# A hybrid diffusion block on one core: modulation and norm in one stage, four modulation rows moved beside the gate projection

## The chip, the cores and the metric

The kernel runs on one core of one Trainium2 chip. Its time is the device time of one execution in microseconds (us), the median of several runs. The core has five engines with queues of their own: TensorE (PE; PEld is its weight load), VectorE (DVE), ScalarE (ACT), GpSimd (POOL) and SyncE (SP, which here only issues DMAs). They wait for each other through semaphores.

## The reference, cut to what matters

The block takes 1024 latent tokens and 256 context tokens of width 1024. Two vectors, `c` for the latents and `c_ctx` for the context, are turned into modulation vectors; the normed tokens are scaled and shifted with them, and one large projection feeds the mixers that follow.

```python
mod = silu(c) @ w_ada + b_ada            # 6 * 1024 values
mod_c = silu(c_ctx) @ w_ada + b_ada
sh1, sc1, g1, sh2, sc2, g2 = split(mod, 6)
csh1, csc1, ... = split(mod_c, 6)
h  = layer_norm(x)   * (1 + sc1)  + sh1
hc = layer_norm(ctx) * (1 + csc1) + csh1
p, pc = h @ w_in, hc @ w_in              # conv channels, q and k, gates, z, v, dt
...                                      # two mixers, merge
x = layer_norm_affine(alpha * x + g1 * y)
h = layer_norm(x) * (1 + sc2) + sh2      # then experts, and g2 in the second residual
```

Only `sh1`, `sc1` and their context twins are needed before the projection. The four vectors `g1`, `sh2`, `sc2`, `g2` are read much later (L2079, L2293), and only those of the latents.

## The kernel before, in words

The program is a row of stages. Each is a block in which every engine has its own program, and a barrier of all engines stands between two stages. The change touches the first three.

`adaln_stage` computes the first 2048 columns of the modulation for `c` and `c_ctx`. `w_ada` comes in four blocks of 512 columns (2 MB each, two buffers). TensorE takes the two silu vectors as stationary (128x2) and streams the weights (L188), so the result is two rows. VectorE adds the bias (L199), GpSimd stores the rows to HBM as `mod` (L205).

`norm_stage` reads these rows back as 32x128, turns them into columns with one transpose (L360), and then works through ten tiles of 128 tokens, two buffers each. For a tile, VectorE takes mean and variance (L302 to L308), ScalarE the root (L340), VectorE normalises (L312), TensorE transposes eight 128x128 squares (L373), VectorE multiplies and adds the modulation columns (L326, L328), ScalarE rounds the result to fp32r, `h_hi` (L345), and VectorE keeps the remainder `h_lo` (L332). Beside the eight latent tiles TensorE computes eight more blocks of 512 modulation columns (L366, L367), ScalarE copies them out (L349), GpSimd stores them (L393).

`project_f_stage` multiplies `w_in` by the tokens: 24 chunks of 128 channels for the convolution, 10 for q and k, 16 for the gates. A chunk's weights (512 KB) come through SP (L465) into one of two buffers; the load waits until the chunk two before has been split. ScalarE rounds them to `w_hi` (L543) once the product two chunks before is done, VectorE keeps `w_lo` (L616), and TensorE makes three passes, hi*hi, hi*lo and lo*hi (L482). For a gate chunk ScalarE applies the Sigmoid (L575) after it has rounded the next chunk's weights, and GpSimd stores it (L685). VectorE does nothing in a gate chunk but the split.

All order is written out by hand in each engine's program, and a queue is served strictly in that order.

Of the kernel before, what the change touches and what calls it, by code (L numbers as in the profile page):

```python
# [23 lines left out]
P = 128  # L24
# [117 lines left out]
def adaln_stage(s, mod):  # L142
# [3 lines left out]
    NB = 2 * D // 512  # L146
    with ExitStack() as st:
        cond = own(st, nc, "cond", [P, 2, KT])
        act_c = own(st, nc, "act_c", [P, 2, KT])
        w = own(st, nc, "w_ada_t", [P, 2, KT, 512])  # L150
        bias = own(st, nc, "b_ada_t", [2, 2 * D])
        row = own(st, nc, "mod_row", [2, 2 * D])
        acc = bank(st, nc, "mod_acc", [P, 2, 512])
        cond_in, bias_in, silu_done = s.sem("cond_in"), s.sem("bias_in"), s.sem("cond_silu")
        w_in = [s.sem(f"ada_w_in{b}") for b in range(2)]

        w_free, acc_free = s.sem("ada_w_free"), s.sem("mod_acc_free")
        stored = s.sem("mod_stored")

        wv = s.x["w_ada"][0].rearrange("(p k) n -> p k n", k=KT)  # L160
        with nc.Block() as block:

            @block.sync
            def _(sp):
                sp.dma_start(cond[:, 0, :], s.x["c"][0].rearrange("(p k) -> p k", k=KT)).then_inc(cond_in, 16)
                sp.dma_start(cond[:, 1, :], s.x["c_ctx"].rearrange("(p k) -> p k", k=KT)).then_inc(cond_in, 16)
                for r in range(2):
                    sp.dma_start(bias[r:r + 1, :], s.x["b_ada"][:, 0:2 * D]).then_inc(bias_in, 16)
                with sp.Fori(0, NB // 2) as i:
                    for b in range(2):  # L170
                        sp.wait_ge(w_free, 2 * i + b + 1)
                        sp.dma_start(w[:, b], wv[:, :, ds(1024 * i + 512 * b, 512)]).then_inc(w_in[b], 16)

            @block.scalar
            def _(act):
                act.wait_ge(cond_in, 32)
                nc.scalar.activation(act_c[:], cond[:], ACT.Silu).then_inc(silu_done, 1)

            @block.tensor
            def _(pe):  # L180
                pe.sem_inc(w_free, 2)
                pe.wait_ge(silu_done, 1)
                with pe.Fori(0, NB // 2) as i:
                    for b in range(2):
                        pe.wait_ge(w_in[b], 16 * i + 16)
                        pe.wait_ge(acc_free, 2 * i + b + 1)
                        for k in range(KT):
# [2528 lines left out]
```

## Time and profile before

| | us |
|---|---|
| median of 3 runs | 3188.68 |
| lowest, highest | 3185.52, 3190.0 |
| the profiled execution | 3189.44 |
| its span | 3187.70 |
| TensorE busy | 2554.5 (80%) |
| VectorE busy | 1654.8 (52%) |
| ScalarE busy | 1024.8 (32%) |
| GpSimd busy | 649.5 (20%) |

In 40 slices of the span (79.7 us each) TensorE's busy share and its granted clock read, in tenths (9 is 90% or more):

```profile
PE   5799999999799747695899669696763888788792
PEclk8999999999899868897999879798876999999996
```

The two stages that become one take nearly the first two slices; slices 9 to 11 hold the gate chunks. The span is measured from the first to the last event of the program, and the execution's own time is 1.74 us longer.

### The profile page before, as it was taken

Reading aid. Unit: us, or ns where it says so; the run is one execution under the profiler, and the core shown is the slowest. Engines: PE = TensorE matmul, PEld = TensorE weight load, DVE = VectorE, ACT = ScalarE, POOL = GpSimd, SP = SyncE. Lnnn points to the kernel's source line nnn. Section 1 sums busy time; section 2 is a strip of 40 time slices with the busy share of each in tenths; the row PEclk is TensorE's granted clock in tenths of the full one; section 3 lists DMA queues with packets and bytes.
Section 4 is the critical chain, followed back from the end, with each engine's and each line's share of the span. In section 5 each row is a group of like instructions: output and inputs, shape, how many; then the busy total and the mean of one; then the engine's idle time right before and its main releaser. Section 6 shows DMA issues by size and latency. Waiting matters only on the chain. (4 is left out here: it accounts for less than half of the span.)

```text
span 3187.7 us, 31676 instructions
## 1 busy us (share of the span) xinstructions
PE 2554.5 (80%) x11173; PEld 1952.1 (61%) x11173; DVE 1654.8 (52%) x1734; ACT 1024.8 (32%) x1231; POOL 649.5 (20%) x462
## 2 busy tenths in 40 slices
PE   5799999999799747695899669696763888788792
PEld 1188888778678612464666358584652767666672
DVE  2545555431010079684566252532655877767775
ACT  0123333121121100352333331311322656555562
POOL 0100001010001149596000000000552121122212
PEclk8999999999899868897999879798876999999996
DMA  5633333343231164895433345444316887788874
GB/s 193 229 98 115 115 115 115 101 147 97 93 125 50 46 238 180 280 309 146 76 72 68 99 139 145 146 139 147 106 59 241 316 325 295 300 317 315 329 292 138
DMA packets 302209, 546.14 MB, mean 171 GB/s; under 512 B 23320, under 2 KB 196872, under 8 KB 279792
## 3 DMA queue, kind: packets, MB, share of 16 engines
q1 hardware_dynamic: 273108, 433.03, 40.3%
q0 software_dynamic: 25440, 91.10, 8.5%
q10 hardware_dynamic: 3584, 21.04, 1.7%
q8 instruction: 41, 0.67, 0.1%
q14 instruction: 36, 0.29, 0.0%
HBM read 425.78 MB, written 119.07 MB: 171 GB/s over the span
## 5 line engine op out<-in xcount | busy, mean ns | idle before, releaser
L2370 DVE TENSOR_TENSOR e_wlo<-e_w,e_whi 128x2048 fp32r<-128x2048 f32 x188 | 426.4, 2289 | 57.9 <-ACT e_whi L2323 57.8
L2323 ACT CAST e_whi<-e_w 128x2048 fp32r<-128x2048 f32 x192 | 366.4, 1915 | 130.1 <-PE e_gu L2483 82.1
L482 PE MATMUL f_lat<-h_hi,w_hi 128*128 128x512 f32 x800 | 254.2, 399 | 0.3 <-DVE w_lo L616 0.3
L482 PE MATMUL f_lat<-h_lo,w_hi 128*128 128x512 f32 x800 | 250.8, 394 | 0.0
L482 PE MATMUL f_lat<-h_hi,w_lo 128*128 128x512 f32 x800 | 250.6, 394 | 0.0
L616 DVE TENSOR_TENSOR w_lo<-w_raw,w_hi 128x1024 fp32r<-128x1024 f32 x50 | 61.2, 1225 | 216.5 <-ACT w_hi L543 216.5
L1918 PE MATMUL b_acc<-b_hi,b_whi 128*128 128x512 f32 x384 | 151.4, 394 | 14.0 <-DVE b_lo L1869 14.0
L1576 PE MATMUL a_c_ps<-a_prob,a_v 128*128 128x512 f32 x304 | 154.6, 592 | 0.0
L482 PEld LDWEIGHTS f_lat<-h_hi,w_hi 128*128 128x128 f32 x800 | 135.9, 188 | 30.4 <-issue 4.8
L482 PEld LDWEIGHTS f_lat<-h_lo,w_hi 128*128 128x128 f32 x800 | 136.0, 188 | 27.6
L482 PEld LDWEIGHTS f_lat<-h_hi,w_lo 128*128 128x128 f32 x800 | 136.0, 188 | 27.7
L629 DVE SCALAR_TENSOR_TENSOR conv_acc<-conv_in,conv_tap_cols,conv_acc 128x1284 f32<-128x1284 f32 x96 | 149.4, 1556 | 3.4
L1918 PE MATMUL b_acc<-b_lo,b_whi 128*128 128x512 f32 x384 | 151.0, 393 | 0.0
L1918 PE MATMUL b_acc<-b_hi,b_wlo 128*128 128x512 f32 x384 | 150.7, 393 | 0.0
L1645 DVE CUSTOM_DVE_ANT_0 a_masked<-a_a_ps,a_mask 128x640 f32<-128x640 f32 x128 | 105.0, 824 | 87.3 <-PE a_a_ps L1549 84.3
L749 PE MATMUL t_acc<-wt_hi,h_hi 128*128 128x512 f32 (+1 forms) x336 | 125.2, 373 | 26.2 <-DVE wt_lo L799 26.2
L2483 PE MATMUL e_gu<-e_whi,e_xhi 128*128 128x512 f32 x512 | 140.3, 396 | 3.2 <-DVE e_xlo L2374 2.4
L2483 PE MATMUL e_gu<-e_wlo,e_xhi 128*128 128x512 f32 x512 | 138.7, 393 | 0.0
L2483 PE MATMUL e_gu<-e_whi,e_xlo 128*128 128x512 f32 x512 | 137.5, 390 | 0.0
L1615 ACT ACTIVATE a_prob<-a_b_ps 128x512 f32<-128x512 f32 x152 | 89.2, 597 | 148.4 <-PE a_b_ps L1565 74.5
L2543 POOL DMA_INDIRECT moe<-e_y,e_scatter_rows x16 | 43.9, 2741 | 429.9 <-DVE e_y L2391 429.9
L749 PE MATMUL t_acc<-wt_hi,h_lo 128*128 128x512 f32 (+1 forms) x336 | 124.8, 372 | 0.0
(323 smaller groups left out, 5313.4 us busy)
## 6 DMA issues: line engine op xcount, KB each, us to landing
e_w<-in_w_gate_up SPq DMA_DIRECT2D x128, 1024.0 KB, 8.5
e_w<-in_w_down SPq DMA_DIRECT2D x64, 1024.0 KB, 5.3
w_raw<-in_w_in SPq DMA_DIRECT2D x50, 512.0 KB, 3.9
w_ada<-in_w_ada SPq DMA_DIRECT2D x8, 2048.0 KB
before<-s_state ACTq DMA_DIRECT2D x16, 1024.0 KB, 3.9
y_before<-before SPq DMA_DIRECT2D x64, 256.0 KB, 6.1
b_w<-in_w_ssd_br SPq DMA_DIRECT2D x16, 1024.0 KB, 5.6
xbcF<-f_out POOLq DMA_DIRECT2D x24, 640.0 KB, 3.4
```

The costliest lines, as they stand in the source:

```text
L482: mm = nc.tensor.matmul(o, weights[:, b, k, :], part[:, k, a:a + n], start=(k == 0 and n_pass == 0), stop=(k == KT - 1 and n_pass == 2))
L616: nc.vector.tensor_tensor(wlo[:, b], w[:, b], whi[:, b].bitcast(F32), ALU.subtract).then_inc(w_free, 1)
L629: nc.vector.scalar_tensor_tensor(conv[:, b], padded[:, b, c:c + W_OUT], tap[:, b, c:c + 1], conv[:, b], ALU.mult, ALU.add).then_inc(conv_s ...
L749: mm = nc.tensor.matmul(acc[:, t % 8, 0:width], part[:, k, a:a + P], weights[:, b, k, 0:width], start=(k == 0 and n_pass == 0), stop=(k == ...
L1576: nc.tensor.matmul(out, values(v, c, g), prob[:, T % PR], start=first, stop=last).then_inc(tiles_summed, 1)
L1615: nc.scalar.activation(prob[:, T % PR], b_ps[:, T % 2], ACT.Exp, scale=SCALE).then_inc(exps_made, 1)
L1645: V.tensor_tensor_reduce(masked[:, h % 2], a_ps[:, h % 2, A0:A0 + KEYS], mask[:, variant(m)], 1.0, NEG, ALU.add, ALU.max, top[:, h:h + 1]) ...
L1918: mm = nc.tensor.matmul(acc[:, b, j], weights[:, b, k, :], xpart[:, k, :], start=(k == ks[0] and n_pass == 0), stop=(k == ks[-1] and n_pas ...
L2323: nc.scalar.copy(whi[:, slot % SPLIT], w[:, slot]).then_inc(w_hi, 1)
L2370: V.tensor_tensor(wlo[:, slot % SPLIT], w[:, slot], whi[:, slot % SPLIT].bitcast(F32), ALU.subtract).then_inc(w_split, 1)
L2483: mm = nc.tensor.matmul(gu[:, 512 * c:512 * c + 512], part[:, b, k, :], weights[:, slot % SPLIT, 512 * c:512 * c + 512], start=(k == 0 and ...
L2543: pool.indirect_dma_start(moe, bass.IndirectOffsetOnAxis(ap=scatter_rows[:, 0:1], axis=0), y[:, b], None, compute_op=ALU.add).then_inc(y_o ...
```

## The change

`adaln_stage` and `norm_stage` become one `front_stage`. All loads are issued at once: four 2 MB blocks of `w_ada`, ten tiles of tokens, each with a place of its own. The modulation is computed the other way round: the weights are the stationary operand (128x128) and the two silu vectors the moving one (128x2), so that it comes out as columns and needs neither HBM nor a transpose. VectorE normalises all ten tiles first, then modulates them with eight instructions of 128x128 per tile, each a multiply and an add with two columns as scalars. ScalarE rounds; the remainder is taken by GpSimd for seven tiles and by VectorE for tiles 2, 5 and 8. Three buffers hold `h` and the transposes.

The four later vectors move into `project_f_stage`, beside the gate chunks, for `c` alone. VectorE adds up `w_ada[:, k] * silu(c)[k]` over eight pieces of 128x1024 (512 KB each, loaded by SP), TensorE sums over partitions with a column of ones, VectorE adds the bias into a row, and SP stores it. Two pieces are handled per gate chunk, a row is finished after chunks 5, 9, 13 and 15 (counted from 0). SP's and TensorE's loops over gate chunks are written out.

```diff
-def adaln_stage(s, mod):
+def front_stage(s, hi, lo):
...
+                load_x(0)
+                load_w(0)
+                sp.dma_start(bias[:], s.x["b_ada"][:, 0:2 * D]).then_inc(bias_in, 16)
+                sp.dma_start(ident[:], s.squares[:, 0:P]).then_inc(ident_in, 16)
+                load_x(1)
+                load_x(2)
+                load_w(1)
+                load_x(3)
+                load_x(4)
+                load_w(2)
+                load_x(5)
+                load_w(3)
+                for n in range(6, NCHUNK):
+                    load_x(n)
...
+                def mods(b):
+                    pe.wait_ge(w_in[b], 16)
+                    for t in range(NT):
+                        kind, j = divmod(b * NT + t, KT)
+                        cols = slice(P * t, P * t + P)
+                        for k in range(KT):
+                            nc.tensor.matmul(mod_ps[:, kind, j, :], w[:, b, k, cols], act_c[:, :, k], start=(k == 0), stop=False)
+                        mm = nc.tensor.matmul(mod_ps[:, kind, j, :], bias[:, 512 * b + P * t:512 * b + P * t + P], ones[:], start=False, stop=True)
+                    mm.then_inc(mods_made, 1)
...
+                for b in range(BLOCKS):
+                    mods(b)
+                    if b < TR:
+                        turn(b)
+                for n in range(TR, NCHUNK):
+                    turn(n)
...
+                centre(NCHUNK - 1)
+                dve.wait_ge(mods_made, BLOCKS)
...
+                    for k in range(KT):
+                        V.tensor_scalar(h[:, n % TR, k, :], tp[:, n % TR, k, :], colm[:, 1, which, k:k + 1], colm[:, 0, which, k:k + 1],
+                                        ALU.mult, ALU.add).then_inc(h_made, 1)
...
+                for n in range(NG):
+                    sp.wait_ge(w_free, NX + NQK + n + 1)
+                    sp.dma_start(w[:, n % 2], wv[:, :, G0 + P * n:G0 + P * n + P]).then_inc(w_in[n % 2], 16)
+                    if n == 0:
+                        load_rest(0)
+                        load_rest(1)
+                    if n >= 1 and 2 * n + 1 < PARTS:
+                        load_rest(2 * n)
+                        load_rest(2 * n + 1)
+                    if n >= 5 and n % 4 == 1:
+                        store_rest(n // 4 - 1)
+                store_rest(REST - 1)
...
+                for n in range(2, NG):
+                    product(NX + NQK + n, n % 2, False)
...
+                    if n >= 5 and n % 4 == 1:
+                        sum_rest(n // 4 - 1)
+                sum_rest(REST - 1)
...
+                for n in range(NG):
+                    if n >= 2:
+                        split_lo(NX + NQK + n, n % 2)
+                    add_rest(2 * n)
+                    add_rest(2 * n + 1)
+                    if n >= 5 and n % 4 == 1:
+                        make_row(n // 4 - 1)
+                make_row(REST - 1)
```

In it `load_rest(j)` loads piece j of `w_ada` into one of two buffers once VectorE has done addition j-2, `store_rest(c)` waits for `make_row(c)` and stores row c, `sum_rest(c)` is TensorE's sum of eight pieces, and `make_row(c)` waits for it.

SP in the gate chunks, before, one turn of the loop over two chunks; `w_raw` is the chunk's weights, `f_w_free` counts the splits:

```order
L465 ISA [waits f_w_free]
L465 DMA w_raw<-in_w_in 128x8x128
L464 REGISTER_ALU
L465 ISA [waits f_w_free]
L465 DMA w_raw<-in_w_in 128x8x128
L462 REGISTER_ALU
L462 COMPARE_AND_BRANCH
```

SP at chunks 5 to 7 now; `f_ada_w` is a piece of `w_ada`, `f_ada_row` the finished row, `f_ada_made` counts rows:

```order
L397 DMA w_raw<-in_w_in 128x8x128 [waits f_w_free]
L385 DMA f_ada_w<-in_w_ada 128x1024 [waits f_ada_step] x2
L393 DMA mod<-f_ada_row 1x1024 [waits f_ada_made]
L397 DMA w_raw<-in_w_in 128x8x128 [waits f_w_free]
L385 DMA f_ada_w<-in_w_ada 128x1024 [waits f_ada_step] x2
L397 DMA w_raw<-in_w_in 128x8x128 [waits f_w_free]
```

The load of chunk 6's weights has come to stand behind two loads of pieces and the store of row 0.

VectorE at the same chunks, before, with the last remainders of the keys ahead of the loop:

```order
L651 TENSOR_TENSOR qk_lo<-f_out,qk_hi 128x1280 [waits f_qk_hi_made] x2
L659 UNCONDITIONAL_BRANCH
L659 ISA
L616 TENSOR_TENSOR w_lo<-w_raw,w_hi 128x1024 [waits f_hi_made]
L615 REGISTER_ALU
L616 TENSOR_TENSOR w_lo<-w_raw,w_hi 128x1024 [waits f_hi_made]
```

And now, from chunk 5's split to chunk 6's; `f_ada_sum` is the running sum, `f_ada_summed` counts TensorE's sums:

```order
L572 TENSOR_TENSOR w_lo<-w_raw,w_hi 128x1024 [waits f_hi_made]
L625 SCALAR_TENSOR_TENSOR f_ada_sum<-f_ada_w,f_act_c,f_ada_sum 128x1024 [waits f_ada_step,f_ada_in0]
L625 SCALAR_TENSOR_TENSOR f_ada_sum<-f_ada_w,f_act_c,f_ada_sum 128x1024 [waits f_ada_step,f_ada_in1]
L632 TENSOR_TENSOR f_ada_row<-f_tp,f_ada_bias 1x1024 [waits f_ada_bias_in0,f_ada_summed]
L572 TENSOR_TENSOR w_lo<-w_raw,w_hi 128x1024 [waits f_hi_made]
```

Between two splits there are now two additions, and at this chunk the row, which waits for TensorE.

TensorE at the start of the program, now; `n_mod_ps` are the modulation columns, `n_tp` the transposes:

```order
L224 MATMUL n_mod_ps<-n_act_c,n_w 128x2 x7
L225 MATMUL n_mod_ps<-n_ones,n_bias 128x2
L224 MATMUL n_mod_ps<-n_act_c,n_w 128x2 x8
L225 MATMUL n_mod_ps<-n_ones,n_bias 128x2
...
L233 MATMUL n_tp<-n_ident,n_x 128x128 [waits n_normed]
L233 MATMUL n_tp<-n_ident,n_x 128x128 x7
L224 MATMUL n_mod_ps<-n_act_c,n_w 128x2 [waits n_w_in1]
```

Where a block of 512 columns was 8 instructions with an output of 2x512, it is now four groups of 8+1 with an output of 128x2, and a tile's transposes stand between two blocks.

## Rows read from the trace of the kernel before

**Rows 1.** The page's busy times: engine, us, share, instructions.

```profile
PE 2554.5 (80%) x11173; PEld 1952.1 (61%) x11173; DVE 1654.8 (52%) x1734; ACT 1024.8 (32%) x1231; POOL 649.5 (20%) x462
```

**Rows 2.** Stretches: length, busy of PE, PEld, DVE, ACT, POOL, clock, DMA share, GB/s.

```profile
10.00:16.40 6.40, 5.03 (x6) 0.73 (x7) 0.00 (x0) 0.00 (x0) 0.00 (x0) 1.00 0.90 343
55.00:165.00 110.00, 83.64 (x244) 26.31 (x245) 67.30 (x98) 19.49 (x31) 8.32 (x15) 0.83 0.66 228
700.00:1000.00 300.00, 273.50 (x1180) 221.81 (x1180) 33.86 (x18) 55.30 (x54) 22.24 (x42) 0.95 0.30 104
```

**Rows 3.** TensorE in order of time, front: start, us, line, names, [idle before].

```profile
11.37 16.36 PE L188 MATMUL mod_acc<-w_ada_t,act_c 128*2 128x512 f32 x32 [11.37 <-DMA w_ada_t<-in_w_ada]
29.44 13.89 PE L188 MATMUL mod_acc<-w_ada_t,act_c 128*2 128x512 f32 x32 [1.71 <-DMA w_ada_t<-in_w_ada]
...
68.49 1.97 PE L373 MATMUL ln_tp<-ident,x_norm 128*128 128x128 f32 x8 [6.29 <-DVE x_norm L312]
...
134.87 7.03 PE L366 MATMUL mod_acc<-w_ada,act_c 128*2 128x512 f32 x16
...
159.65 0.55 PE L482 MATMUL f_ctx<-h_hi,w_hi 128*128 128x256 f32 x1 [16.81 <-DVE w_lo L616]
```

**Rows 4.** The other engines in order of time, between norm and projection.

```profile
144.10 0.52 POOL L393 DMA_DIRECT2D mod<-mod_row  x1 [8.40 <-ACT mod_row L349]
...
146.86 0.33 SPq L457 DMA_DIRECT2D squares<-const_squares  x1
...
157.25 1.04 ACT L543 CAST w_hi<-w_raw 128x1024 fp32r<-128x1024 f32 x1 [13.79 <-DMA w_raw<-in_w_in]
...
158.32 1.23 DVE L616 TENSOR_TENSOR w_lo<-w_raw,w_hi 128x1024 fp32r<-128x1024 f32 x1 [1.14 <-ACT w_hi L543]
```

**Rows 5.** TensorE in order of time, residual stage.

```profile
2243.50 3.60 PE L2054 MATMUL r_logits<-r_router,r_h2F 128*128 128x16 f32 x16 [1.10 <-ACT r_h2F L2104]
...
2247.93 1.05 PE L2041 MATMUL r_acc<-r_wlo,r_mhi 128*128 128x512 f32 x2
...
2252.16 0.63 PE L2041 MATMUL r_acc<-r_whi,r_mhi 128*128 128x512 f32 x2
...
2262.50 1.96 PE L2054 MATMUL r_logits<-r_router,r_h2F 128*128 128x16 f32 x16 [1.10 <-ACT r_h2F L2104]
```

**Rows 6.** Groups by line and form: total us, mean ns of one | idle before.

```profile
L326 DVE TENSOR_TENSOR h_full<-ln_tp,mod_cols 128x1024 f32<-128x1024 f32 x10 | 12.2, 1224 | 0.6 <-PE ln_tp L373 0.3
L1298 DVE TENSOR_SCALAR y_diagonal<-y_squares 128x128 f32<-128x128 f32 x1 | 0.2, 151 | 0.0
L1261 DVE CUSTOM_DVE_ANT_0 y_gdump<-y_g_ps,y_diagonal 128x128 f32<-128x128 f32 x32 | 9.2, 288 | 0.8
L332 DVE TENSOR_TENSOR h_lo<-h_full,h_hi 128x1024 f32 x6 | 7.4, 1226 | 8.4 <-ACT h_hi L345 8.4
L2131 DVE TENSOR_TENSOR r_mlo<-r_m,r_mhi 128x1024 fp32r<-128x1024 f32 x8 | 16.9, 2113 | 17.7 <-ACT r_mhi L2086 17.7
L345 ACT CAST h_hi<-h_full 128x1024 f32 x6 | 6.3, 1046 | 21.2 <-DVE h_full L328 21.2
L2647 POOL TENSOR_TENSOR o_y<-o_y,o_rows 128x1024 f32<-128x1024 f32 x8 | 18.5, 2345 | 26.9 <-DVE o_y L2614 26.9
L2196 POOL TENSOR_TENSOR r_h<-r_h,r_rows 128x1024 f32<-128x1024 f32 x8 | 24.9, 3116 | 0.6
```

**Rows 7.** VectorE, then ScalarE in order of time, at the gate chunks.

```profile
697.62 1.49 DVE L651 TENSOR_TENSOR qk_lo<-f_out,qk_hi 128x1280 fp32r<-128x1280 f32 x1 [3.57 <-ACT qk_hi L581]
...
711.95 1.03 ACT L575 ACTIVATE f_out<-f_lat 128x1024 f32<-128x1024 f32 x1 [9.85 <-PE f_lat L482]
...
723.08 1.02 ACT L575 ACTIVATE f_out<-f_lat 128x1024 f32<-128x1024 f32 x1 [9.16 <-PE f_lat L482]
```

**Rows 8.** L465's landing, 697 to 860; an added VectorE form; a stretch as in rows 2.

```profile
DMA to landing us min/median/max: 3.8/4.0/8.0
...
L2391 DVE SCALAR_TENSOR_TENSOR e_y<-e_down,e_gatec,e_g 128x1024 f32<-128x1024 f32 x16 | 20.5, 1283 | 13.2 <-issue 10.5 <-DVE e_gatec L2387 2.7
...
159.60:163.00 3.40, 3.35 (x10) 2.80 (x11) 1.31 (x2) 0.33 (x1) 0.00 (x0) 0.50 0.58 161
```

More of the change, by code:

```diff
@@ L182, in _ @@
-                pe.wait_ge(silu_done, 1)
[L183 to L187, printed above, removed]
-                            mm = nc.tensor.matmul(acc[0:2, b, :], act_c[:, :, k], w[:, b, k, :],
-                                                  start=(k == 0), stop=(k == KT - 1))
-                        mm.then_inc(w_free, 1)
+                def mods(b):
[7 more added lines that the diff above has]
+                    mm.then_inc(mods_made, 1)
@@ new lines, in centre, with modulate @@
+                def centre(n):
+                    dve.wait_ge(rooted, n + 1)
+                    V.tensor_scalar(x[:, n], x[:, n], mv[:, n, 0:1], root[:, n:n + 1], ALU.subtract, ALU.mult).then_inc(normed, 1)
+                def modulate(n):
+                    which = 1 if n < CCHUNK else 0
+                    dve.wait_ge(turned, n + 1)
+                    if n >= TR:
+                        on_dve, on_pool = split_before(n - TR + 1)
+                        dve.wait_ge(lo_dve, on_dve)
+                        dve.wait_ge(lo_pool, on_pool)
+                    for k in range(KT):
+                        V.tensor_scalar(h[:, n % TR, k, :], tp[:, n % TR, k, :], colm[:, 1, which, k:k + 1], colm[:, 0, which, k:k + 1],
+                                        ALU.mult, ALU.add).then_inc(h_made, 1)
@@ L202, in _ @@
+                V.tensor_scalar(colm[:, 1].rearrange("p r k -> p k r"), mod_ps[:, 1], 1.0, None, ALU.add).then_inc(cols_made, 1)
+                V.tensor_copy(colm[:, 0].rearrange("p r k -> p k r"), mod_ps[:, 0]).then_inc(cols_made, 1)
+                dve.wait_ge(cols_made, 2)
+                for n in range(NCHUNK):
+                    modulate(n)
+                    if n - 1 in ON_DVE:
+                        keep_lo(n - 1)
             @block.gpsimd
             def _(pool):
-                pool.wait_ge(acc_free, NB + 2)
@@ L398, in project_f_stage @@
-def project_f_stage(s, hi, lo, xbcF, xbcT, qkH, qkL, gF):
+                for n in range(NCHUNK):
+                    if n not in ON_DVE:
+                        pool.wait_ge(h_hi, n + 1)
+                        nc.gpsimd.tensor_tensor(lo[:, :, tokens(n)], h[:, n % TR], hi[:, :, tokens(n)].bitcast(F32), ALU.subtract).then_inc(lo_pool, 1)
+def project_f_stage(s, mod, hi, lo, xbcF, xbcT, qkH, qkL, gF):
     nc = s.nc
@@ L442, in project_f_stage @@
         NF = NX + NQK + NG
+        REST = 4
+        PARTS = REST * KT
+        wa = s.x["w_ada"][0].rearrange("(p k) n -> p k n", k=KT)
         def pairs(eng, kind, step):
```

315 lines of the change are left out of this document (117 added, 198 removed).

## The prediction

> **What bounds the kernel now.** I first read the page's busy shares: TensorE is busy 80% of the span [rows 1], but a change at the front must be read from its own stages. The table by stretch comes second [rows 2]: from 55 to 165 us TensorE works 83.64 of 110 us at a mean granted clock of 0.83, and from 700 to 1000, where the gate chunks lie, 273.50 of 300. Third, the front in order of time. TensorE starts at 11.37 when the first 2 MB block of w_ada lands, works until 142 on small transposes and on products with two output rows, and the first product of the projection starts at 159.65 [rows 3]. After the norm stage the last modulation store goes out at 144.10, the projection stage's first load at 146.86, ScalarE rounds the first weights at 157.25 and VectorE has their remainder at 159.55 [rows 4]. So 159.65 us pass before the first projection product. In the gate chunks nothing waits: the Sigmoids of two successive chunks start 11.13 us apart [rows 7], the time of 48 matmuls back to back. Whatever delays a gate chunk is therefore added in full.
>
> **The front.** The two barriers' worth of staging, the trip of the modulation rows through HBM and the four further rows leave; one stage takes their place. Its chain is: w_ada block, TensorE's modulation columns, modulate, split, barrier, tables and weights.
>
> First block: before, it was used at 11.37 [rows 3]; now a tile of x (a quarter of its bytes) is ahead of it, and two small loads must follow it before TensorE starts. I add 1.1: 12.5 us.
>
> Modulation columns: 4 blocks, each 4 x (8+1) = 36 matmuls of fp32 with a 128x128 stationary and two moving columns. At L188 two blocks of 8 fp32 instructions gave 32 records [rows 3], two each, so a block is 72 records. No row has this shape; the nearest is r_logits (128x128 stationary, 16 moving). Sixteen records take 3.60 us at the clock 1.2 GHz, that is (3.60-0.39)/15 = 0.214 us apart, and 1.96 us at 2.4 GHz, 0.113 apart [rows 5]. The spacing is that of the weight load, so fewer moving columns won't shorten it. Which clock holds decides: 15.4 or 8.2 us a block. In the rows the run of r_logits begins at 1.2 GHz after idle time and ends there, and the dense matmuls behind it still start at 1.2; they are at 2.4 from 2252.16 [rows 5], 8.7 us after the run began. The projection, beginning densely at 159.65, is at 1.2 for 3.4 us and then rises [rows 8]. So I take 1.2 GHz for the whole run: 4 x 15.4 = 61.7, plus three turns of 8 transposes between the blocks, 1.97 each at that clock [rows 3] = 5.9. The columns are ready at 12.5+61.7+5.9 = 80.1. At 2.4 GHz after some 5 us it would be 12.5+5+30+3x1.1 = 51. Neither loads nor VectorE end later than that: the 13.6 MB of the stage take 40 us at the 343 GB/s of 10 to 16.4 us [rows 2], and VectorE's normalising is under 67.3-3x12.3 = 30.4 us for all ten tiles [rows 2, 6] and runs beside.
>
> Modulate and split: two copies to columns, 0.7 with their handovers. A tile is 8 instructions of 128x128 out of PSUM. They are not in the trace: at least 0.15 each by a 128x128 without PSUM, at most 0.29 by the custom one [rows 6]. I take 0.21, between them, 1.7 a tile instead of 2 x 1.22. ScalarE's rounding is 1.05, VectorE's subtraction 1.23, GpSimd's 2.35 to 3.12 [rows 6], three buffers, seven tiles on GpSimd. Stepping through: VectorE works 10x1.7+3x1.23 = 20.7, waits some 1.5 for GpSimd's buffers, and behind the last tile come rounding and GpSimd's last subtraction. 24.5 in all (21 to 31), so 105.3.
>
> A rule speaks against this overlap. In r_mlo a VectorE subtraction with two SBUF inputs has a mean of 2.11 beside GpSimd's work against 1.23 where GpSimd has none [rows 6]. The Trainium skill (SBUF — State Buffer, "SBUF: two separate sides") calls the port pair shared by VectorE and GpSimd an exclusive lock for such instructions. By that rule only the three subtractions on VectorE can be blocked, not the modulation out of PSUM: up to 3x0.9 = 2.7 more, inside the 31.
>
> Barrier, tables and weights: from 146.86 to 159.65 it was 12.8; 0.4 for one more load before the weights and 0.3 for the barrier: first product at 105.3+13.5 = 118.8. **Saved: 159.65-118.8 = 40.9 us.**
>
> **The gates.** 32 VectorE instructions of 128x1024 are added, 1.28 each [rows 8]; two per chunk, 2.6 in 11.13, hidden as long as the VectorE has nothing due. What isn't hidden are places at which queues wait in a ring.
>
> (a) Chunks 5, 9 and 13 (the first is 0). SP's order there is: two loads of w_ada, the store of a finished row, and only then the w_in load of the next chunk. The store waits for VectorE's row, the row for TensorE's sum, the sum stands behind the whole product of this chunk. So the next chunk's weights, before loaded a chunk ahead, are now asked for after TensorE has run dry. From the product's end: sum, 4 records of 512 columns at 0.44 (16 take 7.03 [rows 3]) and the drain, 1.9; the row out of PSUM 1.22 [rows 6]; issue of the store 0.4; landing of the weights 4.0 [rows 8]; rounding 1.05 and remainder 1.23 [rows 6]; handovers 0.4: 10.2 us. Queued behind the waiting store are also the next w_ada loads, which nobody misses; behind ScalarE's wait for the weights stands the Sigmoid of this chunk, which TensorE does not need until two chunks on. After 8 us idle the clock falls: restarting costs half of 3.4 to 5 us [rows 5, 8], 2.0. 12.2 x 3 = 36.6.
>
> (b) Chunk 2. SP's second pair of w_ada loads waits for VectorE's first additions, and these stand behind the last key remainder, 697.62 to 699.11 [rows 7]. The w_in load of chunk 2 comes behind: additions end at 699.1+0.8+1.3 = 701.2, issue 702, landing 8.0 (the largest of this stretch, in the same crowd of key and gate stores [rows 8]; at the median it would be 4.0), 710; rounding and remainder 2.4: 712.4, where the product began at 700.3. 12.0 plus 2.0 for the clock = 14.0; with a landing of 4.0, 10.
>
> (c) At the end the fourth sum, row and store (about 6 us) run beside the last Sigmoid and its store: nothing.
>
> **Lost: 36.6+14.0 = 50.6.** Ends for all of it: 38 (stalls of 8.5 and 10, clock 1) and 62 (w_in landing 6 beside the w_ada loads, clock 2.5).
>
> **Sum.** -40.9+50.6 = +9.7. The profiled execution took 3189.44 us (span 3187.70), 0.76 above the median 3188.68 of three; so 3199.1 for it and 3198.4 against the median. I forecast 3198, **slower by 0.3%**. A measurement can tell about 0.2%, 6.4 us, from no change.
>
> **Rivals.**
> A, the clock rises in the modulation columns. For it: L188, with two stationary columns, rises after about 5 us (its first 32 records take 16.36, the next 32 13.89 [rows 3]). Against it: r_logits and the transposes around it, which are of the new kind. Columns at 51, first product at 89.7, saved 70.0, net -19.4: 3169. The Trainium skill (TensorE: Matmul & The Clock Gate, "Part 1: The HAM clock gate") says that the default state is throttled and that activity releases the throttle; read as the engine being occupied, it gives this rival's time, and r_logits in the trace does not bear that reading out. 20%.
> B, the stalls are smaller: SP reaches the w_in load earlier than I read, or it lands in 3.8 and the clock holds. Only the wait for sum and row is left, 1.9+1.2+1.2 = 4.3 at three places, and 10 at chunk 2: lost 23, net -18: 3170. Against it the order of SP is plain. 7%.
> C, heavier: GpSimd's subtractions at 3.12 and the eight small instructions at 0.29 bring the front to 112, the stalls take 62: net +28, 3216. 8%.
> D, the forecast, with 3183 to 3210 as its own range: 65%, of which four fifths are above 3195.
>
> From these: faster by over 0.2% (below 3182.3) 0.27, within 0.2% 0.16, slower 0.57. Range 3170 to 3211.
>
> **What would show it.** In the changed kernel's profile: modulation records about 0.21 us apart and a granted clock of 0.50 from 17 to 80 us; the first modulate at 81, the last remainder near 105, the first projection product near 119. In the gates, TensorE idle four times: 12 us ahead of chunk 2, 8 ahead of 6, 10 and 14, each ended by VectorE's w_lo, this by ScalarE's w_hi, this by the w_in load; after each a clock of 0.50 for 3 to 5 us. Nothing after the gates should differ. I am wrong if the modulation records stand 0.11 apart, or if w_in for chunk 6 is issued before chunk 5's product has ended.

## The result and the profile after

The changed kernel takes 3207.23 us (median of four runs, 3201.33 to 3208.99) against 3189.34 for the kernel before (four runs, 3185.52 to 3192.02). The ratio is 1.0054 with a 95% interval of 1.0036 to 1.0071: slower by 0.54%, 17.9 us. The profiled execution has a span of 3199.7 us and took 3201.33; it is the fastest of the four.

First the page's busy times, columns as in [rows 1]:

```profile
PE 2545.3 (80%) x11268; PEld 2011.8 (63%) x11268; DVE 1682.0 (53%) x1810; ACT 1020.9 (32%) x1223; POOL 656.6 (21%) x460
```

They show nearly nothing of the change: TensorE is even 9.2 us less busy than in [rows 1], yet the kernel is slower. The change is read from the waits and from the order of time.

**The front.** TensorE in order of time, the columns as in [rows 3]. L224 is the modulation product with stationary weights (two moving columns), L225 the bias product behind each group, L233 the transposes of a tile, L423 the projection's product.

```profile
11.38 3.55 PE L224 MATMUL n_mod_ps<-n_act_c,n_w 128*128 128x2 f32 x16 [11.38 <-DMA n_ident<-const_squares]
...
27.43 1.97 PE L233 MATMUL n_tp<-n_ident,n_x 128*128 128x128 f32 x8
...
79.96 0.58 PE L225 MATMUL n_mod_ps<-n_ones,n_bias 1*128 1x2 f32 x2
...
125.47 0.55 PE L423 MATMUL f_ctx<-h_hi,w_hi 128*128 128x256 f32 x1 [23.41 <-DVE w_lo L572]
```

Sixteen groups of 18 records, with three tiles' transposes between them, run without a gap from 11.38 to 80.5. A group takes 3.99 to 4.02 us from start to start (3.85 behind transposes), 0.22 a record, to the end. The first product of the projection starts at 125.47, where it was 159.65 [rows 3]: 34.18 us are saved.

VectorE in order of time behind the columns. L286 takes the first half of them out of PSUM, L272 modulates one 128x128 square, L277 makes a remainder. The last row is GpSimd's last remainder.

```profile
80.58 0.18 DVE L286 TENSOR_SCALAR n_cols<-n_mod_ps 128x16 f32<-128x16 f32 x1 [34.37 <-PE n_mod_ps L225]
...
80.88 10.30 DVE L272 TENSOR_SCALAR n_h<-n_tp,n_cols 128x128 f32<-128x128 f32 x32
91.08 1.23 DVE L277 TENSOR_TENSOR h_lo<-n_h,h_hi 128x1024 fp32r<-128x1024 f32 x1
...
108.65 1.25 DVE L277 TENSOR_TENSOR h_lo<-n_h,h_hi 128x1024 fp32r<-128x1024 f32 x1
...
109.92 2.34 POOL L299 TENSOR_TENSOR h_lo<-n_h,h_hi 128x1024 fp32r<-128x1024 f32 x1 [2.76 <-ACT h_hi L214]
```

VectorE is busy without a gap: 32 instructions in 10.30 us, so 0.32 each. A tile's eight come to 2.58 us, no less than the two wide instructions of the kernel before, 1.22 each [rows 6]. The phase lasts from 80.5 to 112.26.

**The gates.** TensorE's waits between 600 and 910 us (line; waited for; us in total, times, longest):

```profile
PE f_lat L423 <- DVE w_lo L572: 37.6, 4, 13.2
```

One of the four places, chunk 5 to chunk 6, all engines in order of time. L475 is the sum over partitions, L632 makes the row, L393 stores it, L397 loads weights of a gate chunk, L385 the added pieces of w_ada, L499 rounds, L572 makes the remainder.

```profile
727.03 1.88 PE L475 MATMUL f_tp<-f_ada_sum,f_ones 128*1 128x512 f32 x4
...
728.95 1.21 DVE L632 TENSOR_TENSOR f_ada_row<-f_tp,f_ada_bias 1x1024 f32<-1x1024 f32 x1 [18.41 <-PE f_tp L475]
730.19 0.25 SPq L393 DMA_DIRECT2D mod<-f_ada_row  x1
730.48 0.38 SPq L397 DMA_DIRECT2D w_raw<-in_w_in  x1
...
734.68 1.04 ACT L499 CAST w_hi<-w_raw 128x1024 fp32r<-128x1024 f32 x1 [17.64 <-DMA w_raw<-in_w_in]
...
735.76 1.23 DVE L572 TENSOR_TENSOR w_lo<-w_raw,w_hi 128x1024 fp32r<-128x1024 f32 x1 [5.60 <-ACT w_hi L499]
...
737.04 1.22 PE L423 MATMUL f_lat<-h_hi,w_hi 128*128 128x512 f32 x2 [8.13 <-DVE w_lo L572]
```

Read from the bottom up, it is one chain: the product waits for the remainder, the remainder for the rounding, this for a load that SP issues at 730.48, 0.29 behind the store of the row, and the row waits for a sum at the end of the chunk before. The product stands still for 8.13 us behind a sum of 1.88.

The four starts behind a wait (TensorE in order of time, L423), and the first product of the next stage (L732):

```profile
680.23 1.22 PE L423 MATMUL f_lat<-h_hi,w_hi 128*128 128x512 f32 x2 [13.24 <-DVE w_lo L572]
...
794.38 1.22 PE L423 MATMUL f_lat<-h_hi,w_hi 128*128 128x512 f32 x2 [8.09 <-DVE w_lo L572]
...
852.09 1.22 PE L423 MATMUL f_lat<-h_hi,w_hi 128*128 128x512 f32 x2 [8.17 <-DVE w_lo L572]
...
902.23 0.79 PE L732 MATMUL t_acc<-wt_hi,h_hi 128*128 128x512 f32 x1 [24.40 <-DVE wt_lo L782]
```

In the kernel before, chunk 2 starts at 700.38, 540.73 behind the first projection product; now it starts 554.76 behind it: 14.0 more. Of these, 1.06 lie at the start of the projection: the products there come to the spacing of 2.4 GHz 6 us behind the first one, where it was 3.5 before. The other 13.0 are the stop. From one stop to the next there are four chunks. In the kernel before, the Sigmoid thirteen chunks behind the one at 711.95 [rows 7] is this (ScalarE in order of time):

```profile
857.48 1.02 ACT L575 ACTIVATE f_out<-f_lat 128x1024 f32<-128x1024 f32 x1 [10.18 <-PE f_lat L482]
```

So a chunk takes 11.19 on average and four take 44.8. Measured are 56.81 (680.23 to 737.04), 57.34 and 57.71, which is 12.0, 12.6 and 12.9 more; each holds a wait, a sum and the slow clock behind the stop before it. With 14.0 that is 51.5; the rest of the loss, 1.2, is the clock behind the last stop.

Behind each stop the clock is down, in the stretch's row (columns as in [rows 2]):

```profile
737.00:740.60 3.60, 3.56 (x8) 2.81 (x9) 2.75 (x3) 1.05 (x1) 0.53 (x1) 0.50 0.98 275
```

**The balance.** In the kernel before, the next stage's first product starts at 883.67 us (TensorE in order of time):

```profile
883.67 0.79 PE L749 MATMUL t_acc<-wt_hi,h_hi 128*128 128x512 f32 x1 [26.23 <-DVE wt_lo L799]
```

In the changed kernel it starts at 902.23, 18.56 later: 34.18 saved ahead of the projection, 52.74 lost in it. The medians differ by 17.9. The two profiled spans differ by only 12.0. From this product to the end of its span the kernel before takes 2304.0 us and the changed one 2297.5; in the traces of experiments 2, 3, 6, 7 and 8, which leave those stages as they are, it is 2298.7 to 2311.0. So the later stages scatter by some us either way, as whole executions do (the 15 runs of the kernel before beside the first experiments lie between 3177.38 and 3200.43), and I don't explain that part. What a change is worth at its own place is read from the traces up to this product.

### The profile page after: what moved, and what is told of

Its sections match the earlier page's. It is cut to its first block and busy times, and to the rows that moved or that the text cites. A ratio compares the mean times of both kernels' runs of the same rounds, so it can differ in the third digit from the quotient of the medians.

```text
span 3199.7 us, 31530 instructions
## 1 busy us (share of the span) xinstructions
PE 2545.3 (80%) x11268; PEld 2011.8 (63%) x11268; DVE 1682.0 (53%) x1810; ACT 1020.9 (32%) x1223; POOL 656.6 (21%) x460
## 5 line engine op out<-in xcount | busy, mean ns | idle before, releaser
L423 PE MATMUL f_lat<-h_hi,w_hi 128*128 128x512 f32 x800 | 258.6, 405 | 37.6 <-DVE w_lo L572 37.6
L423 PE MATMUL f_lat<-h_lo,w_hi 128*128 128x512 f32 x800 | 254.0, 399 | 0.0
L423 PE MATMUL f_lat<-h_hi,w_lo 128*128 128x512 f32 x800 | 253.2, 398 | 0.0
L423 PEld LDWEIGHTS f_lat<-h_hi,w_hi 128*128 128x128 f32 x800 | 138.2, 192 | 70.8 <-DVE w_lo L572 40.9
L423 PEld LDWEIGHTS f_lat<-h_lo,w_hi 128*128 128x128 f32 x800 | 138.4, 191 | 28.3
L423 PEld LDWEIGHTS f_lat<-h_hi,w_lo 128*128 128x128 f32 x800 | 138.0, 190 | 28.3
L572 DVE TENSOR_TENSOR w_lo<-w_raw,w_hi 128x1024 fp32r<-128x1024 f32 x50 | 61.3, 1226 | 159.9 <-ACT w_hi L499 159.9
L732 PE MATMUL t_acc<-wt_hi,h_hi 128*128 128x512 f32 (+1 forms) x336 | 125.2, 373 | 24.4 <-DVE wt_lo L782 24.4
L732 PE MATMUL t_acc<-wt_lo,h_hi 128*128 128x512 f32 (+1 forms) x336 | 125.0, 372 | 0.0
```

What stands on the lines that cost most here:

```text
L423: mm = nc.tensor.matmul(o, weights[:, b, k, :], part[:, k, a:a + n], start=(k == 0 and n_pass == 0), stop=(k == KT - 1 and n_pass == 2))
L572: nc.vector.tensor_tensor(wlo[:, b], w[:, b], whi[:, b].bitcast(F32), ALU.subtract).then_inc(w_free, 1)
L732: mm = nc.tensor.matmul(acc[:, t % 8, 0:width], part[:, k, a:a + P], weights[:, b, k, 0:width], start=(k == 0 and n_pass == 0), stop=(k == ...
```

## The experiments

All experiments are edits of the changed kernel. The kernel before ran beside them, with a median of 3187.56 us (15 runs) beside experiments 1 to 4 and 3189.74 (ten runs) beside 5 to 8; times of different experiments are compared by their ratios to it. Two theories stood against each other at the gates (ordering of SP's queue, or VectorE's and the DMA engines' added load), and two at the front (what bounds the columns; what makes the modulation dear).

**1. Without the four later rows** (e0_no_rows). The loads, additions, sums and rows are left out, and plain copies of the bias stand in for the four rows.

```diff
@@ SP, gate chunks
-                    if n == 0:
-                        load_rest(0)
-                        load_rest(1)
-                    if n >= 1 and 2 * n + 1 < PARTS:
-                        load_rest(2 * n)
-                        load_rest(2 * n + 1)
-                    if n >= 5 and n % 4 == 1:
-                        store_rest(n // 4 - 1)
-                store_rest(REST - 1)
+                for c in range(REST):
+                    sp.dma_start(mod[0:1, (2 + c) * D:(3 + c) * D], s.x["b_ada"][:, (2 + c) * D:(3 + c) * D]).then_inc(ada_out, 16)
@@ TensorE
-                    if n >= 5 and n % 4 == 1:
-                        sum_rest(n // 4 - 1)
-                sum_rest(REST - 1)
@@ VectorE
-                for n in range(NG):
-                    if n >= 2:
-                        split_lo(NX + NQK + n, n % 2)
-                    add_rest(2 * n)
-                    add_rest(2 * n + 1)
-                    if n >= 5 and n % 4 == 1:
-                        make_row(n // 4 - 1)
-                make_row(REST - 1)
+                for n in range(2, NG):
+                    split_lo(NX + NQK + n, n % 2)
```

> The changed kernel without the four later modulation rows: SP copies the bias into them, so the product with w_ada is left out there. Theory (queues and additions in the gates cost, the front gains): the projection's first product stays at 125.5 us, TensorE is never idle in the gate chunks, and the stretch from there to the next stage's first product is 724.0 us as before the change, not 776.8. The whole is 34 us below the kernel before (3155). Rival (something else in the front or later stages loses the time): the stretch stays over 740 and the kernel is within 15 us of the one before.

Measured: 3151.58 us (four runs), ratio to the kernel before 0.9882 [0.9847, 0.9917]. TensorE's waits between 500 and 910 us, and the next stage's first product:

```profile
PE f_lat L416 <- DVE w_lo L562: 0.2, 1, 0.2
```

```profile
849.12 0.79 PE L716 MATMUL t_acc<-wt_hi,h_hi 128*128 128x512 f32 x1 [26.19 <-DVE wt_lo L766]
```

The 37.6 us of waiting are gone, and the next stage starts 34.55 ahead of the kernel before. From the projection's first product (124.62) to this one it is 724.5 us, as before the change (724.0). The front alone is worth what the trace said, and the loss comes with the added work of the gates; whether by its order or by its load, this run does not tell. The last sum costs nothing: without it the wait at the stage's end is 26.19, as in the kernel before, instead of 24.4; its 1.88 us lay under that wait.

**2. The store of a row one chunk later on SP** (e1_store_later).

```diff
                     if n == 0:
                         load_rest(0)
                         load_rest(1)
+                    if n >= 6 and n % 4 == 2:
+                        store_rest(n // 4 - 1)
                     if n >= 1 and 2 * n + 1 < PARTS:
                         load_rest(2 * n)
                         load_rest(2 * n + 1)
-                    if n >= 5 and n % 4 == 1:
-                        store_rest(n // 4 - 1)
```

> The changed kernel with only SP's order altered: the store of a finished row comes one chunk later, behind the next chunk's weight load. Theory (the weight load is late because it stands behind the store): the idle time before chunks 6, 10 and 14 falls from 8.1 us to about 2.6 (row 1.2 and split 1.2 behind TensorE's sum), the clock stays at 2.4 GHz there, so 3 x (5.5+2) = 22 us less than the changed kernel; the 13.2 us before chunk 2 stay. Rival (the additions and their 16 MB of loads crowd out the weights): the idle time stays above 6 us each and the time within 6 us of the changed kernel.

Measured: 3188.82 us (ten runs, 3181.34 to 3190.08), ratio to the kernel before 1.0002 [0.9989, 1.0016]: by the two ratios 17 us under the changed kernel, in the traces 20 at the next stage's first product (882.27 instead of 902.23). The waits, and the same place as shown above, chunk 5 to 6:

```profile
PE f_lat L423 <- DVE w_lo L572: 20.6, 4, 13.2
```

```profile
729.27 1.21 DVE L632 TENSOR_TENSOR f_ada_row<-f_tp,f_ada_bias 1x1024 f32<-1x1024 f32 x1 [18.40 <-PE f_tp L475]
730.41 1.20 DVE L572 TENSOR_TENSOR w_lo<-w_raw,w_hi 128x1024 fp32r<-128x1024 f32 x1
...
731.67 0.74 PE L423 MATMUL f_lat<-h_hi,w_hi 128*128 128x512 f32 x2 [2.44 <-DVE w_lo L572]
```

Now the weights are there and rounded (717.26) when the sum begins (727.35), and what remains, 2.44, is VectorE: the next chunk's remainder stands behind the row in its program. One move of one store on SP takes three stops from 8.1 us to 2.4. The expected clock of 2.4 GHz came only at the first of them (0.74 for the first two matmuls instead of 1.22). Ahead of chunks 10 and 14 TensorE is idle for the same 2.44, and the granted clock falls all the same, for 3 to 4 us (columns as in [rows 2]):

```profile
780.90:785.00 4.10, 4.01 (x11) 3.16 (x12) 1.03 (x2) 0.00 (x0) 0.00 (x0) 0.58 0.94 304
```

That fits the 20 us of the trace, where 22 were expected. The stop at chunk 2 stays at 13.24, as expected, since its cause is another.

**3. Both orders mended** (e4_gates): SP loads gate weights two chunks ahead of the pieces, VectorE makes the remainder of chunk n+2 before its additions, stores go a chunk later. Nothing is left out.

```diff
-                for n in range(NG):
+                def load_gate(n):
                     sp.wait_ge(w_free, NX + NQK + n + 1)
                     sp.dma_start(w[:, n % 2], wv[:, :, G0 + P * n:G0 + P * n + P]).then_inc(w_in[n % 2], 16)
-                    if n == 0:
-                        load_rest(0)
-                        load_rest(1)
-                    if n >= 1 and 2 * n + 1 < PARTS:
-                        load_rest(2 * n)
-                        load_rest(2 * n + 1)
-                    if n >= 5 and n % 4 == 1:
+
+                load_gate(0)
+                load_gate(1)
+                for n in range(NG):
+                    if n + 2 < NG:
+                        load_gate(n + 2)
+                    load_rest(2 * n)
+                    load_rest(2 * n + 1)
+                    if n >= 6 and n % 4 == 2:
                         store_rest(n // 4 - 1)
...
@@ VectorE
                 for n in range(NG):
-                    if n >= 2:
-                        split_lo(NX + NQK + n, n % 2)
+                    if n + 2 < NG:
+                        split_lo(NX + NQK + n + 2, n % 2)
                     add_rest(2 * n)
                     add_rest(2 * n + 1)
```

> The changed kernel with both queues of the gates reordered: SP issues a chunk's weight load two chunks ahead of the pieces, VectorE splits the chunk after next before its additions, and the stores come a chunk later. Nothing is left out. Theory: no idle time in front of chunks 2, 6, 10, 14; what is left is the three sums of 1.9 us on TensorE; the stretch from the projection's first product to the next stage's is 724+6 = 730 us, and the kernel is 46 us below the changed one, some 28 below the one before (3161). Rival (the additions and their traffic themselves cost): the stretch stays over 745.

Measured: 3162.75 us (six runs), ratio 0.9917 [0.9892, 0.9942]. The waits and the next stage:

```profile
PE f_lat L425 <- DVE w_lo L574: 0.2, 1, 0.2
```

```profile
855.63 0.79 PE L734 MATMUL t_acc<-wt_hi,h_hi 128*128 128x512 f32 x1 [24.37 <-DVE wt_lo L784]
```

With all 16.8 MB of loads, the 32 additions, sums and stores still there, TensorE waits 0.2 us. So neither the bytes nor VectorE's load were the cause, only the order of two queues, SP's and VectorE's. Both orders change in this one run; what each of them gives beyond the store's move is not separated. The next stage starts 6.5 us behind experiment 1: three sums of 1.88 on TensorE's path, 5.6, are most of it.

**4. One increment of eight in place of eight** (e7_one_inc), for the modulation that measured 0.32 us a square.

```diff
                     for k in range(KT):
-                        V.tensor_scalar(...).then_inc(h_made, 1)
+                        ins = V.tensor_scalar(...)
+                    ins.then_inc(h_made, KT)
```

> The changed kernel with one semaphore increment per tile instead of eight in the modulation (the last of the eight instructions adds 8). Theory (the 0.32 us from one 128x128 instruction out of PSUM to the next is the instruction's own fixed cost): the spacing stays at 0.32 and the ten tiles take 25.8 us. Rival (the eight increments cost): the spacing falls to 0.21 or below and the stretch from the first modulation to the last remainder is 8 us shorter.

Measured: 3204.11 us in one run. VectorE's first row of the modulation is as before:

```profile
80.78 10.30 DVE L272 TENSOR_SCALAR n_h<-n_tp,n_cols 128x128 f32<-128x128 f32 x32
```

The spacing does not change, so the semaphore increments are not what makes an instruction dear.

**5. Constants in place of the columns** (e8_constants). The modulation's values are left out: each square is multiplied and added to by constants, everything else runs.

```diff
-                        V.tensor_scalar(h[:, n % TR, k, :], tp[:, n % TR, k, :], colm[:, 1, which, k:k + 1], colm[:, 0, which, k:k + 1],
+                        V.tensor_scalar(h[:, n % TR, k, :], tp[:, n % TR, k, :], 1.5, 0.25,
                                         ALU.mult, ALU.add).then_inc(h_made, 1)
```

> The changed kernel with two constants in place of the two columns as scalars in the modulation, so the modulation's values are left out. Theory (the 0.32 us per instruction is the read of two columns as scalars): the spacing falls to about 0.20 and the ten tiles take 16 us. Rival (it is the cost of a small instruction out of PSUM): it stays at 0.32.

VectorE in order of time:

```profile
81.29 4.84 DVE L272 TENSOR_SCALAR n_h<-n_tp 128x128 f32<-128x128 f32 x24
86.62 1.68 DVE L272 TENSOR_SCALAR n_h<-n_tp 128x128 f32<-128x128 f32 x8 [0.49 <-POOL h_lo L299]
88.21 1.67 DVE L277 TENSOR_TENSOR h_lo<-n_h,h_hi 128x1024 fp32r<-128x1024 f32 x1
```

GpSimd's subtraction beside the last row:

```profile
89.45 2.63 POOL L299 TENSOR_TENSOR h_lo<-n_h,h_hi 128x1024 fp32r<-128x1024 f32 x1 [0.65 <-ACT h_hi L214]
```

The subtractions of the same kernel, GpSimd's and VectorE's (shortest, median and longest in ns, first and last start in us):

```profile
L299 POOL TENSOR_TENSOR h_lo<-n_h,h_hi x7: 2355/2368/2630, 84.1 to 102.0; 128x1024 fp32r<-128x1024 f32 x7
L277 DVE TENSOR_TENSOR h_lo<-n_h,h_hi x3: 1502/1519/1669, 88.2 to 100.8; 128x1024 fp32r<-128x1024 f32 x3
```

24 in 4.84 us: 0.20 each. Reading the two scalars from columns in SBUF is the other 0.12 of the 0.32, for 128 elements a partition. The last remainder ends at 104.4, 8 us earlier, and the projection starts at 116.30 instead of 125.47. The next stage's first product comes at 891.9 instead of 902.23, so the gain lasts through the projection. The single run took 3206.96, so the whole time doesn't show those 9 us; one run of a kernel that scatters by 8 can't, and the claim rests on the trace alone.

**6. Two wide products per group as filler** (e10_filler). Can the clock be raised in the column form? Two extra 512-column matmuls are put ahead of each group.

```diff
+                        for k in range(2):
+                            nc.tensor.matmul(fill_ps[0:2, :], act_c[:, :, k], w[:, b, k, :], start=True, stop=True)
                         for k in range(KT):
                             nc.tensor.matmul(mod_ps[:, kind, j, :], w[:, b, k, cols], act_c[:, :, k], start=(k == 0), stop=False)
```

> The changed kernel with two extra matmuls of 512 columns (two stationary columns, result unused) ahead of each of the 16 groups of modulation matmuls. Theory (the 0.22 us between two records are the weight load at 1.2 GHz, and TensorE is kept there by what it runs): with the clock up, the records stand 0.113 apart, a group takes 2.0+1.7 = 3.7 us instead of 4.0 although it holds more work, and the columns are ready at 71 to 76 us. Rival (the spacing is a fixed cost of this form at either clock): the groups take 1.7 us more each, or 3.4 at 1.2 GHz, and the columns come after 105 us.

Measured: 3243.66 us in one run. The forecast of 71 to 76 for the columns missed by far: they are ready at 110.8. That falls in the number the rival named, but not for the rival's reason, since the clock did rise. TensorE in order of time (L227 is the group without its bias product, L225 the filler), and a stretch's row:

```profile
18.92 3.57 PE L225 MATMUL n_fill_ps<-n_w,n_act_c 128*2 128x512 f32 x4
...
24.77 1.88 PE L225 MATMUL n_fill_ps<-n_w,n_act_c 128*2 128x512 f32 x4
26.57 1.95 PE L227 MATMUL n_mod_ps<-n_act_c,n_w 128*128 128x2 f32 x16
...
31.46 3.58 PE L227 MATMUL n_mod_ps<-n_act_c,n_w 128*128 128x2 f32 x16
```

```profile
60.00:100.00 40.00, 40.00 (x153) 21.00 (x152) 0.00 (x0) 0.00 (x0) 0.00 (x0) 0.67 0.00 1
```

A group takes 1.95 us at 2.4 GHz and 3.58 at 1.2, by the spacing that the prediction took from [rows 5]. But TensorE, busy for all of the 40 us, is granted 0.67 on average: the clock rises and falls again and again. The filler, four records a group, costs 3.57 us at the lower level and 1.88 at the upper, more than the clock gave back.

The same rows compare the two forms of the product. A block of 512 columns is 16 records like the filler's, or 64 like the group's: 4 x 3.57 = 14.3 against 4 x 3.58 = 14.3 us at 1.2 GHz, and 7.5 against 7.8 at 2.4. At one clock the two cost nearly the same.

**7. The front with the weights streamed** (e5_front_rows). Silu's vectors stand still, w_ada streams past in 512 columns; ScalarE keeps each row of 512, and four transposes of 2x128 turn it to columns. The rest is the changed kernel.

```diff
                 def mods(b):
                     pe.wait_ge(w_in[b], 16)
+                    if b >= 1:
+                        pe.wait_ge(rows_kept, b)
+                    for k in range(KT):
+                        nc.tensor.matmul(row_ps[0:2, :], act_c[:, :, k], w[:, b, k, :], start=(k == 0), stop=False)
+                    nc.tensor.matmul(row_ps[0:2, :], ones[:], bias[:, 512 * b:512 * b + 512], start=False, stop=True).then_inc(rows_made, 1)
+
+                def to_columns(b):
+                    pe.wait_ge(rows_kept, b + 1)
                     for t in range(NT):
                         kind, j = divmod(b * NT + t, KT)
-                        cols = slice(P * t, P * t + P)
-                        for k in range(KT):
-                            nc.tensor.matmul(mod_ps[:, kind, j, :], w[:, b, k, cols], act_c[:, :, k], start=(k == 0), stop=False)
-                        mm = nc.tensor.matmul(mod_ps[:, kind, j, :], bias[:, 512 * b + P * t:512 * b + P * t + P], ones[:], start=False, stop=True)
+                        mm = nc.tensor.transpose(mod_ps[:, kind, j, :], row[:, P * t:P * t + P], ident[0:2, 0:2])
                     mm.then_inc(mods_made, 1)
```

> The changed kernel with only the modulation turned round again: the two silu vectors stationary, the weights streamed as in L188 and L366, the two rows kept by ScalarE and turned into columns with four transposes of 2x128 per block. Nothing is left out. Theory (the front is bound by 288 weight loads at 1.2 GHz): the columns are ready by the end of VectorE's normalising, at 46 us instead of 80.5, the first projection product comes at 91, and the kernel is 34 us below the changed one (3173). Rival (loads or VectorE bound the front as well): the first product comes later than 110.

Measured: 3180.68 us (seven runs), ratio 0.9968 [0.9952, 0.9984]. TensorE in order of time, L235 the streamed product, L250 the tile's transposes, L242 the small ones; the last row is VectorE's first copy:

```profile
11.40 9.07 PE L235 MATMUL n_row_ps<-n_w,n_act_c 128*2 128x512 f32 x16 [11.40 <-DMA n_ident<-const_squares]
...
21.35 1.09 PE L250 MATMUL n_tp<-n_ident,n_x 128*128 128x128 f32 x8
22.71 7.03 PE L235 MATMUL n_row_ps<-n_w,n_act_c 128*2 128x512 f32 x16
...
49.88 0.40 PE L242 MATMUL n_mod_ps<-n_ident,n_row 2*128 2x2 f32 x4 [0.67 <-ACT n_row L216]
...
50.32 0.18 DVE L304 TENSOR_SCALAR n_cols<-n_mod_ps 128x16 f32<-128x16 f32 x1 [3.01 <-PE n_mod_ps L242]
```

A block of 16 records takes 7.03, as in the kernel before [rows 3]. With its bias product it is 7.9 us from 22.71 to the next transposes, where the column form takes 4 x 4.0 = 16.0 with its own. The engine reaches 2.4 GHz inside the first block and the transposes take 1.09 instead of 1.97. By the rows of experiment 6 nearly all of the difference is the clock: at 1.2 GHz the streamed block would be as long as the other. The columns are ready at 50.3 instead of 80.5, the projection starts at 94.30 instead of 125.47. Expected were 46 and 91, and 3173 for the whole: the gain is some 27 us by the two ratios, where 34 were expected. In the trace the next stage's first product comes at 870.3, 32 ahead of the changed kernel; the rest lies in the scatter of the later stages.

**8. Experiments 3 and 7 together** (e6_both).

> The turned modulation and the reordered gate queues together, nothing left out. Theory (front and gates are independent): both gains add, 34 us below the kernel with the reordered gates (3162.75), so 3129, 59 below the kernel before. Rival (an earlier front is given back later): above 3145.

Measured: 3134.14 us (four runs, 3130.63 to 3140.78), ratio 0.9821 [0.9799, 0.9842]: 1.8% faster than the kernel before, and by the two ratios 74 us under the changed one. The first projection product, and the next stage's:

```profile
94.78 0.55 PE L443 MATMUL f_ctx<-h_hi,w_hi 128*128 128x256 f32 x1 [22.90 <-DVE w_lo L592]
...
824.30 0.79 PE L752 MATMUL t_acc<-wt_hi,h_hi 128*128 128x512 f32 x1 [24.30 <-DVE wt_lo L802]
```

59.4 us ahead of 883.67 in the trace, 55.6 by the medians, where 59 were expected. The two repairs add up: each works at its own place.

## Why the prediction held, and where it was off

The forecast was slower by 0.3% at 3198 us; measured were 0.54% and 3207.23. The sign and the mechanism were right, and the time lies inside the range, 4 us below its upper end and 9 above the forecast. The size of the change was not met: 0.3% lies under the measured interval of 0.36% to 0.71%. In the trace the sum of +9.7 came out as +18.6; 6.7 of the 8.9 missing are the front, by one mis-sized term (modulate and split), and 2.1 the gates. The chances given to C and D make 0.60 for slower (0.08 and four fifths of 0.65), where the summary has 0.57. By its steps:

- **First block**, forecast 12.5: measured 11.38. The tile of x and the small loads delay nothing; the identity table is the last to arrive, when the first block did before.
- **Modulation columns**, forecast 80.1: measured 80.5. The 1.1 us gained at the start was used up by blocks of 15.9 to 16.05 instead of 15.4 (four of which are 61.6, not 61.7). The row with sixteen moving columns held for two (16 records in 3.60 and 3.58); the 0.214 took 0.39 off it for the last record, which was too much, since the records start 0.22 apart. The clock stayed at 1.2 GHz to the end of the run of 69 us. Rival A, the clock rising, had 20% and did not come about. A sign that I named for the forecast was wrong in one point: the granted clock's column reads 1.00 from 17 to 80 us, not 0.50. The records are the evidence, 0.22 apart against 0.12 in experiment 6, and the transposes, 1.97 against 1.09 in experiment 7. The stretch's row (columns as in [rows 2]):

```profile
17.00:80.00 63.00, 63.00 (x287) 62.54 (x286) 18.62 (x44) 1.53 (x8) 0.00 (x0) 1.00 0.33 132
```

- **Modulate and split**, forecast 25.2 with the copies, to 105.3: measured 31.7, to 112.26. This is the mis-sized term. The prediction took 0.21 an instruction, bounds 0.15 and 0.29; it was 0.32, above both, so that ten tiles cost 25.8 us instead of 16.8. Experiment 5 shows why: 0.20 with constants, 0.32 with two columns as scalars, and none of the rows I took the bounds from read such columns. With constants the phase ended at 104.4. Of the 9 us more some came back, since a slower VectorE did not have to wait for GpSimd's buffers, where I had 1.5. The upper end that I gave, 31 and 0.7 for the copies, was just reached.
- **The rule on the shared port**, up to 2.7 more: the changed kernel could not show it. VectorE's three remainders took 1.23 to 1.25 (L277), but none ran beside GpSimd: they end at 92.31, 101.10 and 109.90, and GpSimd's next subtractions start at 92.34, 101.13 and 109.92. In experiment 5 they do overlap, by 0.7 to 1.0 us each, and took 1.67, 1.52 and 1.50, and GpSimd's subtractions up to 2.63 instead of 2.35. So the two do slow each other when they meet. The modulation out of PSUM ran beside GpSimd and kept its spacing of 0.32.
- **Barrier, tables and weights**, forecast 13.5: measured 13.2 (112.26 to 125.47).
- **Saved**, forecast 40.9: measured 34.2, all of the gap in the modulation.
- **Chunks 5, 9 and 13**, forecast 12.2 each, of which 8.3 of waiting, 1.9 sum and 2.0 clock: measured 12.0, 12.6 and 12.9, with waits of 8.09 to 8.17 and sums of 1.88. What remains, 2.0 to 2.9, is mostly the clock. Experiment 2 shows the cause of the waits: with the store moved they are 2.4. The prediction let the clock fall after 8 us of idling; in experiment 2 it fell at two of three stops of 2.44 as well.
- **Chunk 2**, forecast 12.0 and 2.0 for the clock: measured 14.0 to its start, 13.0 without the slower start of the projection, and the clock behind it. The choice of 8.0 over 4.0 for the landing was right and still short. The load is issued at 668.46 and rounded at 677.87, 9.4 later (SP, then ScalarE in order of time):

```profile
668.46 0.48 SPq L397 DMA_DIRECT2D w_raw<-in_w_in  x1
...
677.87 1.04 ACT L499 CAST w_hi<-w_raw 128x1024 fp32r<-128x1024 f32 x1 [13.41 <-DMA w_raw<-in_w_in]
```

Landings of all 16 of these loads, against [rows 8]:

```profile
DMA to landing us min/median/max: 4.0/6.5/9.4
```

Two pieces of w_ada go out right ahead of nearly each, and the median is 6.5 instead of 4.0 ([rows 8] has those from 697 to 860 alone). It matters only where the load is late.
- **The end**, forecast nothing: experiment 1 shows it, the last sum lies under the wait of the next stage.
- **Lost**, forecast 50.6: measured 52.7. Rival B (4.3 a stop) is out by the trace; C named 62 and the front at 112, of which the front's mechanism was half right (the small instruction was dearer) and the gates' was not.

What the prediction had right about the structure was found in the code's order, not in a share: the gate chunks had no slack, so each thing that a queue put ahead of a weight load came out in full. What it did not consider is that the form with stationary weights was the worse one at the front, because the clock stayed down under it: with streamed weights the columns are ready 30 us earlier.

## What to carry to other kernels

Where a stage has TensorE busy without a gap, added side work costs what it puts on TensorE itself (here three sums of 1.88 us), and nothing more only if no queue serving that stage waits for it: put the loads that the main work needs ahead of every wait for the side work, on SP and on VectorE alike, and a store that waits for a result of this step into the next one. Here the product with two vectors was cheaper with the vectors stationary and the weights streamed, because the clock rose under it; turning a row of 512 values to columns cost TensorE 0.4 us, and 0.7 of waiting for ScalarE's copy where nothing lay between (the last block). Before a form is chosen, look in a trace at the clock that it runs at. When sizing a missing instruction, look for a row with the same kinds of operands, not only the same size.

## What the runs showed of the hardware

- VectorE's tensor-scalar on 128x128 fp32 out of PSUM: 0.20 us with constants, 0.32 with two columns of SBUF as scalars.
- TensorE, fp32 with a 128x128 stationary and two moving columns: 0.22 us a record at 1.2 GHz, 0.12 at 2.4. From 17 to 80 us the weight load was busy for 62.54 of 63.00 us, and sixteen moving columns took the same as two, so the weight load sets it. A run of such products without a gap stayed at 1.2 GHz for 69 us, and filled up with wide ones it went up and down (0.67 on average). The products that stream 512 columns reached 2.4 GHz within 10 us.
- The profile's clock column read 1.00 in that run, at the start of the program, while the records' spacing is that of 1.2 GHz. At the start the column is to be checked against a known row.
- After stops of the same length (2.44 us idle behind a sum of 1.88) the granted clock stayed at 1.00 once and fell to the level of 1.2 GHz twice, for 3 to 4 us (experiment 2).
- A VectorE subtraction of 128x1024 with two SBUF inputs took 1.23 to 1.25 us alone and 1.50 to 1.67 where it met GpSimd's for 0.7 to 1.0 us.
